# The step from attention to the merge stage, cut into channel tiles, with row splits, stores and head sums moved between stages and engines

## The chip, the cores and the metric

One core of one Trainium2 chip runs the whole program once. The metric is device time in microseconds (us), the median over executions; a profile of one further execution gives the rows that are shown. The engines are TensorE (PE; PEld is its weight load), VectorE (DVE), ScalarE (ACT), GpSimd (POOL) and SyncE (SP), which here only issues transfers.

## The reference, cut to what matters

A decoder block: sixteen meta tokens are put ahead of 2048 tokens of 1024 channels; a convolution branch and an attention branch are computed from the same projection, merged, and followed by a mixture of experts. The stages around the change compute this:

```python
a = silu(layernorm(a, ln_g, ln_b))          # convolution branch, 512 channels
y_conv = a @ w_conv_out + b_conv_out
o = forgetting_attention(q, k, v, logf).reshape(B, L, 512)   # 8 heads of 64
y_attn = o @ w_attn_out
merged = sigmoid(gate_c) * y_conv + sigmoid(gate_a) * y_attn
```

The layer norm runs over the 512 channels of a token. The attention's softmax is divided out late: the attention stage leaves unscaled head outputs and, per head and token, the sum of the exponentials, whose reciprocal scales the heads in the merge stage.

## The kernel before, in words

The program is five stages, one after the other: project, attend, merge, route, experts. A stage is a block with one instruction stream per engine; the next block begins when all engines have left it. Engines wait for each other by semaphores, in the order in which the code issues the instructions. Float32 products are made of two halves: a matrix is split into a high half (rounded for TensorE, on ScalarE) and a low half (the rest, on VectorE), and `pair_matmuls` makes three matmuls of one product (lines 92 to 94).

**Attend** (`stage_attend`). Four pairs of heads, each with 32 units (two heads by 16 query tiles of 128 tokens), each unit in groups of up to 512 keys. Per group TensorE transposes the probabilities (`turn`), ScalarE copies the high half (`high`), VectorE subtracts the low half (`low_part`), and three groups later TensorE multiplies by the values (`times_values`). At every second unit ScalarE copies a finished output (`take_output`) and GpSimd adds its two halves and, once per head, stores it to `o_d` in DRAM. The last pair's last four units (28 to 31; 3, 2, 3 and 3 groups) have no further scores to make, and into them is laid the layer norm of the first chunk of 512 tokens of the convolution branch, which lies in `conv` as four channel tiles of 128 x 512: `means` on TensorE gives the mean, VectorE subtracts it, ScalarE squares, `means` gives the variance, ScalarE takes the root, VectorE the reciprocal in two parts (line 1322). After the last group VectorE inverts the row sums (line 1332), TensorE turns them, VectorE scales all of `conv` at once (1334), ScalarE applies SiLU tile by tile (1272) and copies the high half of all four tiles (1276), and VectorE subtracts the low half (1339). SP stores the inverted sums and waits for that store.

**Merge** (`stage_merge`). Four chunks of 512 tokens. A chunk is 16 products (`PRODUCTS`) of 12 matmuls each: eight for `y_conv` (from `s_hi`, `s_lo`) and eight for `y_attn` (from `o_hi`, `o_lo`), into four PSUM banks in turn; the first four products of the first chunk go row block by row block (`first_products`). The eight row blocks of the two weights (`w_rooms`) are split at the start: `high(k)` on ScalarE (1515), `low(k)` on VectorE (1567). VectorE takes each product through its gate (`gated`, 1577, 1582, 1584), which frees its bank. Between these takes it works for what comes next, by a schedule written by hand over the product number i: `heads_and_halves` adds the two halves of the head outputs loaded from `o_d` (`add_heads`, 1590), scales them (1595) and splits off the low half (1600) for this chunk; `statistics` makes the layer norm of the next chunk's `conv`: sum over the four channel tiles by one strided reduction (`sum_tiles`, 1608), TensorE's `mean` (1459), `centre`, the square's sum, `invert`, `scale`, and at i = 13 `low_conv` for all four tiles. SP loads the heads of the next chunk at i = 7 and its `conv` at i = 13. GpSimd does nothing in this stage but one subtraction in its last chunk (2369).

## Time and profile before

| | |
|---|---|
| device time, 3 runs | median 2576.16 us (2573.84 to 2580.01) |
| the profiled execution | 2576.4 us; its span, first to last instruction, 2574.8 us |
| mean granted TensorE clock | 0.98 of full |
| busy share of the span | PE 95%, PEld 78%, DVE 73%, ACT 42%, POOL 20% |
| merge stage, first to last matmul | 1386.56 to 1591.96 us from the start of the span |

PE's busy share counts matmuls that wait in its pipeline, so it overstates TensorE. Times in the rows are counted from the start of the span. In a timeline the bracket says how long the engine sat idle before the row, and what ended that.

### The profile page before, as it was taken

How to read it: one execution, taken by the hardware profiler on the slowest of the kernel's cores; microseconds unless marked ns; L12 is line 12 of the kernel's file. 1: busy time of each engine (PE TensorE's matmuls, PEld its weight loads, DVE VectorE, ACT ScalarE, POOL GpSimd, SP SyncE). 2: the span in 40 equal slices, each digit the busy share in tenths (PEclk: the TensorE clock that was granted, in tenths of full speed). 3: DMA queues.
4: the chain of work that ended last, by engine and by line, in shares of the span. 5: the costliest groups of instructions: out<-in, count | busy, mean ns of one | idle time of the engine just before them, and what ended most of it. 6: DMA issues, size and time to landing. Idle time of an engine off the chain costs nothing. (4 is left out here: it accounts for less than half of the span.)

```text
span 2574.8 us, 33570 instructions
## 1 busy us (share of the span) xinstructions
PE 2440.4 (95%) x12296; PEld 2002.0 (78%) x12296; DVE 1881.9 (73%) x2422; ACT 1072.7 (42%) x1556; POOL 515.2 (20%) x477
## 2 busy tenths in 40 slices
PE   6999999999999999999996899999399999999998
PEld 6899898999988888989884777777367777677664
DVE  7699999799311078888886776466588888888773
ACT  6101001455212167878774222323255555555540
POOL 1222212111101101111110001011324443233221
PEclk9999999999999999999998999999699999999999
DMA  5111112232325153364424677536389999999986
GB/s 174 41 58 58 66 47 68 83 124 83 122 91 159 49 150 100 103 171 109 118 83 123 192 212 250 199 132 232 135 314 358 372 364 366 371 371 369 360 319 202
DMA packets 180273, 469.86 MB, mean 182 GB/s; under 512 B 33573, under 2 KB 104579, under 8 KB 145548
## 3 DMA queue, kind: packets, MB, share of 16 engines
q1 hardware_dynamic: 133202, 371.64, 42.4%
q0 software_dynamic: 31120, 49.48, 5.7%
q10 hardware_dynamic: 15794, 46.67, 4.8%
q8 instruction: 96, 1.57, 0.3%
q14 instruction: 61, 0.50, 0.1%
HBM read 408.65 MB, written 118.29 MB: 205 GB/s over the span
## 5 line engine op out<-in xcount | busy, mean ns | idle before, releaser
L92 PE MATMUL project_bank<-project_xnT_hi,project_w_hi 128*128 128x512 f32 (+4 forms) x1352 | 499.6, 370 | 0.7 <-DVE project_work L796 0.6
L93 PE MATMUL project_bank<-project_xnT_lo,project_w_hi 128*128 128x512 f32 (+4 forms) x1352 | 498.2, 368 | 0.0
L94 PE MATMUL project_bank<-project_xnT_hi,project_w_lo 128*128 128x512 f32 (+4 forms) x1352 | 496.4, 367 | 0.0
L809 DVE SCALAR_TENSOR_TENSOR project_work<-project_work,project_taps 128x2048 f32<-128x2048 f32 x128 | 335.5, 2621 | 4.5
L92 PEld LDWEIGHTS project_bank<-project_xnT_hi,project_w_hi 128*128 128x128 f32 (+1 forms) x1352 | 251.2, 186 | 29.8 <-issue 1.5
L94 PEld LDWEIGHTS project_bank<-project_xnT_hi,project_w_lo 128*128 128x128 f32 (+1 forms) x1352 | 251.3, 186 | 26.6
L93 PEld LDWEIGHTS project_bank<-project_xnT_lo,project_w_hi 128*128 128x128 f32 (+1 forms) x1352 | 251.1, 186 | 26.6
L2736 PE MATMUL experts_y_bank<-weights_down,experts_hT 128*128 128x512 f32 x544 | 245.9, 595 | 0.6 <-ACT experts_hT L2789 0.6
L1302 DVE TENSOR_TENSOR attend_pT<-attend_t_bank,attend_pT 128x512 fp32r<-128x512 f32 (+3 forms) x352 | 213.8, 613 | 35.4 <-ACT attend_pT L1236 34.5
L1169 PE MATMUL attend_o_bank<-attend_pT,attend_values 128*128 128x256 f32 x1216 | 225.2, 304 | 6.7 <-DVE attend_pT L1302 6.7
L1236 ACT ACTIVATE attend_pT<-attend_t_bank 128x512 fp32r<-128x512 f32 (+3 forms) x352 | 184.2, 539 | 89.6 <-PE attend_t_bank L1155 86.8
L92 PE MATMUL experts_gu_bank<-weights_high,experts_xT_hi 128*128 128x512 f32 x512 | 215.1, 420 | 6.6 <-DVE weights_low L2379 4.2
L595 ACT ACTIVATE project_work<-project_bank,project_params 128x512 f32<-128x512 f32 x64 | 44.0, 690 | 393.3 <-PE project_bank L94 393.3
L93 PE MATMUL experts_gu_bank<-weights_low,experts_xT_hi 128*128 128x512 f32 x512 | 202.6, 396 | 0.0
L94 PE MATMUL experts_gu_bank<-weights_high,experts_xT_lo 128*128 128x512 f32 x512 | 201.8, 394 | 0.0
L2379 DVE TENSOR_TENSOR weights_low<-weights_room,weights_high 128x2048 fp32r<-128x2048 f32 x86 | 193.0, 2284 | 0.0
L1155 PE MATMUL attend_t_bank<-first_ident,attend_probs 128*128 128x128 f32 x1216 | 190.3, 273 | 0.8 <-DVE attend_pT L1302 0.3
L2736 PEld LDWEIGHTS experts_y_bank<-weights_down,experts_hT 128*128 128x128 f32 x544 | 103.4, 191 | 105.4 <-issue 98.9
L407 POOL CAST project_w_hi<-project_w_raw 128x1024 fp32r<-128x1024 f32 (+1 forms) x35 | 44.4, 1267 | 697.9 <-PE project_bank L94 697.9
L2778 ACT ACTIVATE experts_xT_hi<-experts_x_bank 128x1024 fp32r<-128x1024 f32 x64 | 65.7, 1027 | 277.9 <-PE experts_x_bank L2697 277.9
L1169 PEld LDWEIGHTS attend_o_bank<-attend_pT,attend_values 128*128 128x128 f32 x1216 | 167.8, 190 | 9.2 <-DVE attend_pT L1302 8.6
L1155 PEld LDWEIGHTS attend_t_bank<-first_ident,attend_probs 128*128 128x128 f32 x1216 | 148.6, 140 | 25.1 <-issue 3.9
(320 smaller groups left out, 4693.9 us busy)
## 6 DMA issues: line engine op xcount, KB each, us to landing
weights_down<-in_w_down_dram SPq DMA_DIRECT2D x68, 1024.0 KB, 9.0
weights_room<-in_w_gate_dram SPq DMA_DIRECT2D x45, 1024.0 KB, 9.6
weights_room<-in_w_up_dram SPq DMA_DIRECT2D x45, 1024.0 KB, 14.4
weights_third<-in_w_gate_dram SPq DMA_DIRECT2D x23, 1024.0 KB, 9.7
weights_third<-in_w_up_dram SPq DMA_DIRECT2D x23, 1024.0 KB, 14.6
project_w_raw<-in_w_in_dram SPq DMA_DIRECT2D x36, 512.0 KB, 4.4
qk_d<-project_work SPq DMA_DIRECT2D x16, 1032.0 KB, 5.4
gate_d<-project_work ACTq DMA_DIRECT2D x16, 1024.0 KB, 4.2
```

The source lines that it names most:

```text
L92: pe.matmul(out, lhs[0], rhs[0], start=first, stop=False)
L93: pe.matmul(out, lhs[0], rhs[1], start=False, stop=False)
L94: return pe.matmul(out, lhs[1], rhs[0], start=False, stop=last)
L407: nc.gpsimd.tensor_copy(w_hi[:, b, :, 0:width], w_raw[:, b, :, 0:width]).then_inc(w_hi_ready, 1)
L809: nc.vector.scalar_tensor_tensor(out=work[:, 2, 0:SEQ], in0=work[:, 1, META - 1 + q:META - 1 + q + SEQ], scalar=taps[:, bass.ds(ct, 1), q] ...
L1155: m = nc.tensor.transpose(t_bank[:, j % 3, (t % 4) * P:(t % 4 + 1) * P], probs[:, u % BUF, t * P:(t + 1) * P], ident[:, :])
L1169: m = nc.tensor.matmul(out, values[:, h, t, :], pT[:, j % (LAG + 1), t % 4].rearrange("p k q -> p (k q)"), start=t == 0, stop=t == last)
L1236: nc.scalar.activation(pT[:, j % (LAG + 1), 0:n, 0, :], t_bank[:, j % 3, 0:n * P].rearrange("p (t q) -> p t q", q=P), ACT.Copy)\
L1302: nc.vector.tensor_tensor(pT[:, j % (LAG + 1), 0:n, 1, :], t_bank[:, j % 3, 0:n * P].rearrange("p (t q) -> p t q", q=P), raw(pT[:, j % (LA ...
L2379: nc.vector.tensor_tensor(self.low[n % 2][:, cut, :, :].rearrange("p c k n -> p k c n"), self.gate_up_rooms[n % 3][:, :, cut, :], raw(self ...
L2736: m = nc.tensor.matmul(y_bank[:, b, half, :], hT[:, b, c, :], down_raw[r][:, c, cols], start=c == 0, stop=c == HC - 1)
L2778: nc.scalar.activation(xT_hi[:, b, :, :], x_bank[:, :, :].rearrange("p k (c t) -> p (k c) t", t=P), ACT.Copy).then_inc(x_hi_ready, 1)
```

## The change

- **Tail of attention.** The first chunk's centring and squaring come one or two groups earlier, the variance's `means` one group later; the row sums are inverted at unit 29 and turned at unit 31; the reciprocal of the root comes in four parts instead of two. ScalarE and VectorE split weight rows 0 and 1 in units 29 and 30.
- **Seam.** The scaling, SiLU, high half and low half of the first chunk go by channel tile. Only tile 0 is scaled in the attend block; the rest is in the merge block, among the splits of weight rows 2 and 3, and each matmul row block waits for its own tile.
- **Stores.** The last pair's last two sums and the last store of `o_d` go from the attend block into the merge block on GpSimd; the store of the inverted sums is no longer waited for in attend. In merge SP waits for these stores, then loads the heads, and the next `conv` after them instead of ahead.
- **Merge chunks.** GpSimd adds the heads' halves in all four chunks. The strided reduction becomes two additions (128 x 1024 and 128 x 512). Scaling and low half go by tile. In the first chunk the statistics move from products 0 to 13 to products 7 to 15 and their two `mean` matmuls from among the convolution products to among the head products; the next `conv` is loaded at i = 15. In later chunks the first sum moves from i = 0 to i = 1.

```diff
+    def high_w(self, nc, k):
+        nc.scalar.activation(self.w_hi[:, k, :], self.w_rooms[k % 6], ACT.Copy).then_inc(self.w_hi_ready, 1)
+
+    def low_w(self, nc, k):
+        nc.vector.tensor_tensor(self.w_lo[:, k, :], self.w_rooms[k % 6], raw(self.w_hi[:, k, :]), ALU.subtract)\
+          .then_inc(self.w_ready, 1)
+
+    def scale_tile(self, nc, t, inv_root):
+        nc.vector.tensor_tensor(self.conv[:, t, :], self.conv[:, t, :], inv_root, ALU.mult).then_inc(self.scaled, 1)
...
-            sp.dma_start(inv_d.rearrange("h (t q) -> (h t) q", q=P), inv_rows[:, :]).then_inc(inv_stored, 16)
-            wait(sp, inv_stored, 16)
+            sp.dma_start(inv_d.rearrange("h (t q) -> (h t) q", q=P), inv_rows[:, :]).then_inc(merge.inv_stored, 16)
...
+            with pool.Fori(0, PAIRS - 1) as it:
+                sums(it, UNITS)
...
+            sums(PAIRS - 1, UNITS - 2)
...
+                    if not more and (u, g) == (UNITS - 1, 0):
+                        pe.wait_ge(inv_done, 1)
+                        nc.tensor.transpose(s_bank[:, 2, 0:P], inv_sum[:, :], ident[:, :]).then_inc(inv_done, 1)
+                    if not more and (u, g) == (UNITS - 2, 1):
                         pe.wait_ge(merge.squared, 1)
...
-                    if not more and (u, g) == (UNITS - 3, 0):
+                    if not more and (u, g) == (UNITS - 4, 1):
...
+                    if not more and (u, g) in ((UNITS - 3, 1), (UNITS - 2, 0)):
+                        wait(act, merge.w_loaded[u - (UNITS - 3)], 16)
+                        merge.high_w(nc, u - (UNITS - 3))
+                    if not more and (u, g) == (UNITS - 2, 0):
                         wait(act, merge.var_done, 1)
...
-            wait(act, merge.param_loaded, 48)
...
-            m.then_inc(merge.silu_done, 1)
-            wait(act, merge.silu_done, 1)
-            nc.scalar.activation(merge.s_hi[:, :, :], merge.conv[:, :, :], ACT.Copy).then_inc(merge.s_hi_ready, 1)
...
+                    if not more and (u, g) == (UNITS - AHEAD, 0):
+                        dve.wait_ge(merge.mean_done, 1)
+                        nc.vector.tensor_tensor(merge.conv[:, :, :], merge.conv[:, :, :],
+                                                over_channels(s_bank[:, 0, :]), ALU.subtract)\
+                          .then_inc(merge.centred, 1)
                     low_part(it, u, g)
...
-                    if not more and u == UNITS - 1 and g < 2:
+                    if not more and (u, g) == (UNITS - 3, 1):
+                        dve.wait_ge(exp_done, PAIRS * UNITS + 2)
+                        nc.vector.reciprocal(inv_sum[:, :], row_sum[:, :]).then_inc(inv_done, 1)
+                    if not more and (u, g) == (UNITS - 2, 0):
+                        for k in range(2):
+                            wait(dve, merge.w_hi_ready, k + 1)
+                            merge.low_w(nc, k)
+                    if not more and (u, g) in INVERT_AT:
+                        n = INVERT_AT.index((u, g))
                         dve.wait_ge(merge.root_ready, 1)
-                        nc.vector.reciprocal(inv_root[:, 256 * g:256 * (g + 1)], root[:, 256 * g:256 * (g + 1)])\
+                        nc.vector.reciprocal(inv_root[:, P * n:P * (n + 1)], root[:, P * n:P * (n + 1)])\
...
-            dve.wait_ge(exp_done, PAIRS * UNITS + 2)
-            nc.vector.reciprocal(inv_sum[:, :], row_sum[:, :]).then_inc(inv_done, 1)
-            dve.wait_ge(merge.inv_ready, 2)
-            nc.vector.tensor_tensor(merge.conv[:, :, :], merge.conv[:, :, :], over_channels(inv_root), ALU.mult)\
...
+            dve.wait_ge(merge.inv_ready, 4)
+            merge.scale_tile(nc, 0, inv_root)
             dve.wait_ge(inv_done, 2)
-            nc.vector.tensor_copy(inv_rows[:, :], t_bank[:, 0, 0:P]).then_inc(inv_done, 1)
-            dve.wait_ge(merge.s_hi_ready, 1)
-            nc.vector.tensor_tensor(merge.s_lo[:, :, :], merge.conv[:, :, :], raw(merge.s_hi[:, :, :]), ALU.subtract)\
-              .then_inc(merge.s_lo_ready, 1)
+            nc.vector.tensor_copy(inv_rows[:, :], s_bank[:, 2, 0:P]).then_inc(inv_done, 1)
...
-            wait(sp, merge.s_lo_ready, 1)
-            merge.load_conv(sp, 1)
-            load_heads(0)
             for k in (6, 7):
                 wait(sp, w_ready, k - 5)
                 merge.load_w(sp, k)
+            wait(sp, merge.inv_stored, 16)
+            for s in merge.o_stored:
+                wait(sp, s, 16 * PAIRS)
+            load_heads(0)
+            wait(sp, merge.s_lo_ready, CT)
+            merge.load_conv(sp, 1)
...
+                    if i == PRODUCTS - (1 if first else 3) and more and not (isinstance(c, int) and c == TC - 2):
+                        wait(sp, merge.s_lo_ready, c * CT + 2 * CT)
...
+                    if i == 0:
+                        pe.wait_ge(merge.s_lo_ready, c * CT + (j + 1))
                     m = part(i, j, r, hi, lo)
...
-                    if t == 3 and more:
+                    if t == 3 and more and not first:
...
+                    if t == 1 and first:
+                        mean(1, 0, merge.mean_done)
+                    if t == 4 and first:
+                        mean(2, 1, merge.var_done)
...
+            tiles, o_raw, o_sb, o_tile = merge.last_sums
+            for n, i in enumerate(tiles):
+                halves = o_raw[:, 2 * P * n:2 * P * (n + 1)]
+                nc.gpsimd.tensor_tensor(o_sb[:, i * P:(i + 1) * P], halves[:, 0:P], halves[:, P:2 * P], ALU.add)\
+                  .then_inc(o_sums, 1)
+            wait(pool, o_sums, 2)
+            pool.dma_start(o_tile, o_sb.rearrange("p (c n) -> p c n", n=512)).then_inc(merge.o_stored[1], 16)
+
+            for c in range(TC):
+                wait(pool, o_loaded, c * 96 + 96)
+                for half in range(2):
+                    s = slice(2 * half, 2 * half + 2)
+                    nc.gpsimd.tensor_tensor(o_top[:, s, :], o_top[:, s, :], o_low[:, s, :], ALU.add)\
+                      .then_inc(o_added, 1)
...
+            def conv_tile(c, t):
+                wait(act, merge.scaled, c * CT + (t + 1))
+                nc.scalar.activation(conv[:, t, :], conv[:, t, :], ACT.Silu, bias=merge.ln[:, 1, t:t + 1],
+                                     scale=merge.ln[:, 0, t:t + 1]).then_inc(merge.silu_done, 1)
+                wait(act, merge.silu_done, c * CT + (t + 1))
+                nc.scalar.activation(s_hi[:, t, :], conv[:, t, :], ACT.Copy).then_inc(merge.s_hi_ready, 1)
...
-                    square(c + 1)
+                square(c + 1)
...
+                wait(act, y_done, c * PRODUCTS + DC)
...
-                wait(act, y_done, c * PRODUCTS + DC)
-                nc.scalar.activation(s_hi[:, :, :], conv[:, :, :], ACT.Copy).then_inc(merge.s_hi_ready, 1)
-
-            for k in range(6):
+                    conv_tile(c + 1, t)
+
+            wait(act, merge.param_loaded, 48)
+            conv_tile(0, 0)
+            conv_tile(0, 1)
+            high(2)
+            conv_tile(0, 2)
+            high(3)
+            conv_tile(0, 3)
+            for k in range(4, W_CHUNKS):
...
-                nc.vector.tensor_reduce(over_tiles[:, :], source[:, :, :].rearrange("p t n -> p n t"), AX.X, ALU.add)\
+                nc.vector.tensor_tensor(squares[:, 0:2, :], source[:, 0:2, :], source[:, 2:4, :], ALU.add)\
+                  .then_inc(tiles_summed, 1)
+                wait(dve, merge.inv_ready, n // 2 + 3)
+                wait(dve, tiles_summed, n * 2 - 1)
+                nc.vector.tensor_tensor(over_tiles[:, :], squares[:, 0, :], squares[:, 1, :], ALU.add)\
...
+                wait(dve, merge.inv_ready, c + 4)
+                for t in range(CT):
+                    merge.scale_tile(nc, t, inv_root[:, :])
+
+            def low_conv(c, t):
+                wait(dve, merge.s_hi_ready, c * CT + (t + 1))
+                nc.vector.tensor_tensor(s_lo[:, t, :], conv[:, t, :], raw(s_hi[:, t, :]), ALU.subtract)\
                   .then_inc(merge.s_lo_ready, 1)
...
-                    if i in (4, 5):
-                        add_heads(0, i - 4)
-                        scale_heads(0, i - 4)
-                    elif i == 6:
-                        low(CT + 2)
-                        low(CT + 3)
-                    elif i == 7:
+                    if i == 3:
+                        for half in range(2):
+                            scale_heads(0, half)
+                    elif i == 5:
                         low_heads(0, 0)
...
-                    add_heads(c, i - 1)
                     scale_heads(c, i - 1)
...
-                if i == 0 and not first:
+                if i == (7 if first else 1):
                     sum_tiles(conv, merge.conv_loaded, c * 16 + 32, c * 2 + 1)
-                elif i == (1 if first else 3):
+                elif i == (9 if first else 3):
                     centre(c + 1)
-                elif i == (3 if first else 5):
+                elif i == (10 if first else 5):
                     sum_tiles(squares, merge.squared, c + 2, c * 2 + 2)
-                elif i == 8:
+                elif i == (12 if first else 8):
                     invert(c + 1)
-                elif i == 9:
+                elif i == (13 if first else 9):
                     scale(c + 1)
+                elif first and i >= 14:
+                    low_conv(1, 2 * i - 28)
+                    low_conv(1, 2 * i - 27)
                 elif i == 13:
-                    low_conv(c + 1)
+                    for t in range(CT):
+                        low_conv(c + 1, t)
 
...
-            for k in range(CT):
+            for t in range(1, CT):
+                merge.scale_tile(nc, t, merge.first_inv_root)
+            low_conv(0, 0)
+            low_conv(0, 1)
+            for k in (2, 3):
                 low(k)
+                low_conv(0, k)
+            for k in range(CT, W_CHUNKS):
+                low(k)
+            for s in merge.o_stored:
+                wait(dve, s, 16 * PAIRS)
```

## Rows read from the trace of the kernel before

**Rows 1.** PE's timeline over the merge stage: last attention product, waits, first matmuls of chunks.
```profile
1371.80 0.58 PE L1169 MATMUL attend_o_bank<-attend_pT,attend_values 128*128 128x256 f32 x1 [1.07 <-DVE attend_pT L1302]
...
1386.56 0.77 PE L92 MATMUL merge_y_bank<-merge_s_hi,merge_wm_hi 128*128 128x512 f32 x1 [13.43 <-DVE merge_wm_lo L1567]
...
1421.17 0.80 PE L92 MATMUL merge_y_bank<-merge_o_hi,merge_wm_hi 128*128 128x512 f32 x1 [8.17 <-DVE merge_o_lo L1600]
...
1445.03 0.40 PE L92 MATMUL merge_y_bank<-merge_s_hi,merge_wm_hi 128*128 128x512 f32 x1
...
1470.36 1.12 PE L1459 MATMUL merge_stat_bank<-merge_over_tiles,merge_mean_w 128*128 128x512 f32 x2 [1.97 <-DVE merge_over_tiles L1608]
...
1493.13 0.40 PE L92 MATMUL merge_y_bank<-merge_s_hi,merge_wm_hi 128*128 128x512 f32 x1
...
1522.25 2.07 PE L1459 MATMUL merge_stat_bank<-merge_over_tiles,merge_mean_w 128*128 128x512 f32 x2 [4.02 <-DVE merge_over_tiles L1608]
...
1547.63 0.40 PE L92 MATMUL merge_y_bank<-merge_s_hi,merge_wm_hi 128*128 128x512 f32 x1
...
1591.57 0.39 PE L94 MATMUL merge_y_bank<-merge_o_hi,merge_wm_lo 128*128 128x512 f32 x1
```

**Rows 2.** Windows view, seam: engine busy times and counts, granted clock, DMA share, GB/s.
```profile
1380.00:1390.00 10.00, 3.44 (x8) 2.79 (x9) 7.06 (x6) 6.77 (x7) 0.00 (x0) 0.50 0.54 163
```

**Rows 3.** Timeline, DVE and ACT, from attention's end to the next stage's first split.
```profile
1372.52 2.23 DVE L1334 TENSOR_TENSOR merge_conv<-merge_conv,attend_scores 128x2048 f32<-128x2048 f32 x1
...
1374.82 1.28 ACT L1272 ACT_TABLE_LOAD   x1 [1.75 <-DVE merge_conv L1334]
...
1376.12 2.93 ACT L1272 ACTIVATE merge_conv<-merge_conv,merge_ln 128x512 f32<-128x512 f32 x4
...
1379.08 1.91 ACT L1276 ACTIVATE merge_s_hi<-merge_conv 128x2048 fp32r<-128x2048 f32 x1
1381.02 2.29 DVE L1339 TENSOR_TENSOR merge_s_lo<-merge_conv,merge_s_hi 128x2048 fp32r<-128x2048 f32 x1 [6.08 <-ACT merge_s_hi L1276]
...
1384.14 2.00 ACT L1515 ACTIVATE merge_wm_hi<-merge_wm_raw 128x1024 fp32r<-128x1024 f32 x2 [3.16 <-PEq L985]
```

**Rows 4.** Timeline, PE and DVE, in attention's last units.
```profile
1356.71 5.40 PE L1181 MATMUL attend_s_bank<-attend_scores,merge_mean_w 128*128 128x512 f32 x8 [2.67 <-ACT attend_scores L1261]
...
1367.65 1.74 DVE L1322 RECIPROCAL attend_scores<-attend_scores 128x256 f32<-128x256 f32 x1
...
1371.51 0.23 DVE L1302 TENSOR_TENSOR attend_pT<-attend_t_bank,attend_pT 128x128 fp32r<-128x128 f32 x1
```

**Rows 5.** Groups by line, DVE in merge: busy us, mean ns, idle before.
```profile
L1608 DVE TENSOR_REDUCE merge_over_tiles<-merge_conv 128x512 f32<-128x2048 f32 x2 | 7.7, 3847 | 1.0 <-DMA merge_conv<-conv_d 1.0
L1584 DVE TENSOR_TENSOR merge_m_sum<-merge_m_sum,merge_prod_a 128x512 f32<-128x512 f32 x9 | 6.2, 692 | 0.4
L1590 DVE TENSOR_TENSOR merge_o_top<-merge_o_top,merge_room 128x1024 f32<-128x1024 f32 x4 | 4.8, 1208 | 0.0
```

**Rows 6.** POOL's timeline at the end of attention: the last sums and their store.
```profile
1373.25 2.21 POOL L1118 TENSOR_TENSOR attend_o_sb<-attend_o_raw 128x128 f32<-128x128 f32 x2 [4.71 <-ACT attend_o_raw L1244]
1376.19 0.77 POOL L1122 DMA_DIRECT2D o_d<-attend_o_sb  x1 [0.73 <-POOL attend_o_sb L1118]
```

**Rows 7.** DMA view, windows holding single issues at 1376.19, 1383.57, 1387.14: KB, us to landing.
```profile
o_d<-attend_o_sb POOLq DMA_DIRECT2D x1, 1024.0 KB, 4.4
merge_conv<-conv_d SPq DMA_DIRECT2D x1, 1024.0 KB, 5.2
merge_room<-inv_d SPq DMA_DIRECT2D x1, 512.0 KB, 16.8
```

**Rows 8.** GpSimd's large additions by group, and two tiles' minimum/median/maximum ns.
```profile
L2369 POOL TENSOR_TENSOR weights_merged_lo<-weights_merged_lo,weights_merged_hi 128x1024 fp32r<-128x1024 f32 x1 | 2.4, 2399 | 187.6 <-ACT weights_merged_hi L2365 187.6
L409 POOL TENSOR_TENSOR project_w_lo<-project_w_raw,project_w_hi x35: 317/2626/4344, 69.8 to 862.7; 128x1024 fp32r<-128x1024 f32 x34, 128x64 fp32r<-128x64 f32 x1
L809 DVE SCALAR_TENSOR_TENSOR project_work<-project_work,project_taps x128: 2350/2352/4385, 93.4 to 447.8; 128x2048 f32<-128x2048 f32 x128
```

84 lines of the change are left out of this document (24 added, 60 removed).

## The prediction

> **What bounds the kernel now.** I read four views: the windows and PE's timeline to find where TensorE stands still, the other engines' timelines to see who releases it, the groups by line for durations, the DMA view for loads that moved. Four things are to be seen.
>
> First, between the last attention product at 1371.80 and the first merge matmul at 1386.56 TensorE has one small transpose to do [rows 1]. The chain is serial, over whole 128 x 2048 tiles: scaling 2.23, table load 1.28, four SiLUs 2.93, high half 1.91, low half 2.29 us, then the change of block, from 1383.31 to ScalarE's first split at 1384.14, 0.83 us [rows 3], then the first row's split.
>
> Second, in the first chunk TensorE finishes its convolution products at 1413.00 and waits 8.17 us for the heads' low half until 1421.17 [rows 1].
>
> Third, chunk lengths. The last chunk, which prepares no successor, runs from 1547.63 to 1591.96: 44.3 us, so 0.231 us a matmul. The others take 58.5, 48.1 and 54.5 us. Chunks 1 and 2 stop for the sum over channel tiles, 1.97 and 4.02 us [rows 1], behind reductions of 3.85 us on VectorE [rows 5]. Chunk 1 less its wait is 46.1, which is the 44.3 plus 1.8 for two `mean`s.
>
> Fourth, the clock. After a stop the granted clock is 0.50 of full, the 1.2 GHz level [rows 2], and the first matmuls come at half pace: the eight head products of the first chunk, restarted at 1421.17, take 23.9 us to 1445.03 instead of 22.2 [rows 1].
>
> Everything after merge waits for it by events, so I carry a gain at the last merge matmul through to the end.
>
> **The change, part by part.** I follow one time line, in us of the trace.
>
> *Tail.* The centring moves into a stretch in which VectorE is idle, and the row sums' reciprocal moves ahead of the last groups. Against that VectorE gets two splits of about 1.2 us (a row of the same size [rows 5]), and ScalarE two high halves of 1.0 [rows 3]. They lie beside `means`, which takes 5.40 us from 1356.71 [rows 4]; TensorE has nothing for them to do then. After `means`, VectorE's chain is five low parts (about 2.7 us in all) and four reciprocals of half the 1.74 us [rows 4], about 6.3 us, beginning 1.4 us after `means`. With `means` starting at about the same 1356.8 and taking 3.7 us at full clock or 5.4 at half, the last low part ends between 1368 and 1369.8, against 1371.74 now [rows 4]. Tile 0's scaling (a quarter of 2.23) and the copy of the inverted sums follow, beside the last output's copy. The merge block begins at 1370.8 (bounds 1369.8 and 1372.5, the latter if nothing of the tail is saved).
>
> *Seam.* What is left ahead of the first matmul: table load 1.28, one SiLU 0.73, one high half a quarter of 1.91 and some start-up, 0.55, one low half 0.6, hops 0.2. The first row's split is done already. 1370.8 + 3.4 = 1374.2, against 1386.56: 12.3 us (bounds 10.5 and 13.5). Tiles 1 to 3 and rows 2 and 3 come from ScalarE in turns of about 1.3 and 1.0 us, while TensorE spends at least 2.8 us, and 5.1 at half clock, on a row block: covered, the last tile is there at about 1381. Without that cover each tile would cost its 1.3.
>
> One rule of the Trainium skill (ScalarE: Activation LUTs, What ACT_TABLE_LOAD costs) adds a drain of 1.38 us to each table load. The rows show the SiLU starting 0.02 us after the load's 1.28, and the load 0.07 us after its releaser [rows 3]; with the page's figure the first matmul would stand at 1375.6. The sum goes by the row.
>
> *The heads.* The old order had the store out at 1376.19, landed 4.4 later, and loads from 1383.94 behind a `conv` load [rows 6, 7]. Now GpSimd's two sums begin with the block: 0.9 to 2.2 us [rows 6] (2.2 where VectorE scales meanwhile; I take 1.5), 0.7 to the issue, 4.4 to landing: 1377.5. SP's issues then queue behind this wait: six head loads, then `conv`, and with it the first gates. The two weight loads go out first and land before 1377. The head loads: `conv` landed at 1383.57 + 5.2 = 1388.8, the last head load at 1387.14 + 16.8 = 1403.9, so 3 MB took 15.1 us [rows 7]. From 1377.8, with 2 us of start-up, they land at 1395 (bounds 1393 and 1398).
>
> Then two GpSimd additions of 128 x 1024. The same form took 2.40 us where VectorE did other things, 2.63 at the median and up to 4.34 in the project stage [rows 8]. I take 2.4 here (VectorE waits idle for them) up to 3.2: 1399.8. Scaling two halves, high halves, two takes and two low halves, 1.2 us each, follow on VectorE: 6.3 us. The head products start at 1406 (bounds 1403 and 1409), against 1421.17. TensorE ends its convolution products at 1374.2 plus the old 26.4 us less two `mean`s, 1.8: 1398.8, so it stands still for 7 us here, and the slow clock after it stays as it was.
>
> *End of the first chunk.* 1406 + 23.9 + 1.8 for the `mean`s moved here = 1431.7. But the statistics of chunk 1 are now compressed into products 7 to 15. I followed them: takes of 1.4 us (twice 0.69 [rows 5]), centre 2.3, square 1.9, sum 1.9, root, reciprocal 3.5, scaling 2.3 bring the scaled tile 0 to about 1430, SiLU and high half of it to 1432, and the low halves of tiles 0 to 3 to 1434 to 1438.5 between two takes. TensorE, waiting tile by tile, loses 4.8 us (bounds 2 and 8). Chunk 1's effective start is 1436.5, against 1445.03: 8.5 us ahead.
>
> *Chunks 1 and 2.* VectorE loses the additions, 2 x 1.21, and 2 x (3.85 - 1.9) of reductions [rows 5]: 6.3 us of about 40 a chunk. The waits of 1.97 and 4.02 go, and in chunk 2 the slow clock behind the second: ideal is 46.1 each. Against that stand GpSimd's additions. The DVE operation with two SBUF inputs that takes 2.35 us at the median took up to 4.39 while GpSimd made its additions [rows 8]: each side can hold the other for up to one operation. Here the loads land near the end of a chunk, where VectorE makes the next chunk's low halves. Two additions of 2.4 can hold it for 0 to 4.8 us; I take 1.3 on TensorE's path. Chunk 2's `conv` lands late as before and costs 0.6. So 47.4 and 48.0: gains 0.7 and 6.5. Chunk 3 stays 44.3.
>
> *Sum.* 8.5 + 0.7 + 6.5 = 15.7, so 16 us. The profiled 2576.4 less 16 is 2560.4; its distance to the median of 2576.16 is 0.2 us, nothing here. A change under 0.2%, 5 us, counts as none.
>
> **Rivals.**
>
> *The chain holds everywhere (0.22).* No boundary stall beyond 2 us at chunk 1 and no interference: 8.5 + 2.8 + 2.0 + 8.4 = 21.7, to 2555. For it: the tile-wise waits let TensorE start on tile 0. Against it: the compressed statistics above.
>
> *GpSimd and VectorE hold each other (0.16).* Additions take 3.2 us, so the heads come 1.6 us later, and the starts of chunks 1 and 2 lose 3.2 us each beyond the sum: 16 - 8 = 8, to 2568. For it: the 4.39 and 4.34 [rows 8]. Against it: many VectorE operations in merge read PSUM and one SBUF operand. [...]
>
> *The other side (0.05).* GpSimd's eight additions fall on the path throughout. At the longest row, 4.34, they cost 34.7 where VectorE spent 9.7 [rows 5, 8]: 25 us lost against the 21.7, slower by 3, to 2580. It decides from 3.9 us an addition, with all eight on the path. Against it: six of the eight are requested long before their sums are used.
>
> *The change gains nothing (0.04).* The stage's start could still hang on something that this trace hides behind the VectorE chain, as the barrier's wait for the store of the sums, landing at 1380.6 [rows 6, 7]; with the heads late behind it, 2574 to 2578.
>
> **How the numbers follow.** My forecast has 0.53, at 2560.4, its own range 2555.5 to 2565. The range of 2552 to 2569 takes in the first two rivals and the bounds: best case 13.5 - 12.3 + 21.7 = 23, with 1 for run to run; worst 8 less 1. It leaves out some 0.15. Faster by over 0.2% 0.91, within 0.04, slower 0.05.
>
> **What the changed profile would show.** The first merge matmul comes near 1374.2, some 5 us behind the last attention product instead of 14.8. The head products start near 1406 with a wait named for VectorE's `o_lo` and behind it GpSimd's additions. Chunk 1 begins with waits on single `s_lo` tiles, 3 to 6 us in sum. Chunks 1 and 2 last 47 to 48 us with no wait of 4 us for the channel sum and no half clock. GpSimd's additions last 2.4 us, and some of VectorE's tile operations (0.6) are stretched to 2 or 3. The prediction is wrong if the head loads land after 1400, if the barrier is later than 1373, or if the stretch at the chunk boundaries exceeds 5 us each.

## The result, and the profile after

The changed kernel takes 2562.39 us in the median of 7 runs (2556.7 to 2569.27), the kernel before, beside it on the same chip, 2578.75 us (7 runs, 2573.84 to 2582.92). The ratio is 0.9938, with a 95% interval of 0.9923 to 0.9953: 0.6% faster. The profiled execution took 2561.39 us with a span of 2559.6, against the 2574.8 of before, so the trace shows 15.2 of the 16 us. The forecast was 2560.4 us, 15.7 less than before.

PE's timeline of the changed kernel, with the rows that answer to [rows 1] and [rows 4]:

```profile
1356.84 3.60 PE L1204 MATMUL attend_s_bank<-attend_scores,merge_mean_w 128*128 128x512 f32 x8
...
1367.37 0.58 PE L1192 MATMUL attend_o_bank<-attend_pT,attend_values 128*128 128x256 f32 x1 [0.26 <-DVE attend_pT L1320]
...
1373.11 0.77 PE L92 MATMUL merge_y_bank<-merge_s_hi,merge_wm_hi 128*128 128x512 f32 x1 [5.16 <-DVE merge_s_lo L1670]
...
1405.17 0.80 PE L92 MATMUL merge_y_bank<-merge_o_hi,merge_wm_hi 128*128 128x512 f32 x1 [7.50 <-DVE merge_o_lo L1641]
...
1434.83 0.50 PE L92 MATMUL merge_y_bank<-merge_s_hi,merge_wm_hi 128*128 128x512 f32 x1 [4.42 <-DVE merge_s_lo L1670]
...
1437.97 0.80 PE L92 MATMUL merge_y_bank<-merge_s_hi,merge_wm_hi 128*128 128x512 f32 x1 [0.28 <-DVE merge_s_lo L1670]
...
1484.51 0.40 PE L92 MATMUL merge_y_bank<-merge_s_hi,merge_wm_hi 128*128 128x512 f32 x1
...
1530.35 0.40 PE L92 MATMUL merge_y_bank<-merge_s_hi,merge_wm_hi 128*128 128x512 f32 x1
...
1533.79 0.50 PE L92 MATMUL merge_y_bank<-merge_s_hi,merge_wm_hi 128*128 128x512 f32 x1 [1.18 <-DVE merge_s_lo L1670]
...
1575.74 0.39 PE L94 MATMUL merge_y_bank<-merge_o_hi,merge_wm_lo 128*128 128x512 f32 x1
```

The stop at the seam is 5.16 us instead of 13.43, and the waits for the channel sums are gone: 1.97 in chunk 1, 4.02 in chunk 2, and one of 1.46 in chunk 2 that [rows 1] leave out. The stop ahead of the head products is still there, 7.50 us for 8.17, and a new one of 4.42 us stands at chunk 1's first matmul. The last merge matmul ends at 1576.13.

The seam on ScalarE and VectorE, as [rows 3] of before, timeline view:

```profile
1367.23 0.68 DVE L973 TENSOR_TENSOR merge_conv<-merge_conv,attend_decay 128x512 f32<-128x512 f32 x1
...
1369.52 1.28 ACT L1562 ACT_TABLE_LOAD   x1 [0.87 <-PEq L1003]
1370.81 0.81 ACT L1562 ACTIVATE merge_conv<-merge_conv,merge_ln 128x512 f32<-128x512 f32 x1
1371.66 0.63 ACT L1565 ACTIVATE merge_s_hi<-merge_conv 128x512 fp32r<-128x512 f32 x1
...
1372.32 0.69 DVE L1670 TENSOR_TENSOR merge_s_lo<-merge_conv,merge_s_hi 128x512 fp32r<-128x512 f32 x1 [0.92 <-ACT merge_s_hi L1565]
```

One tile's chain, 1.28, 0.81, 0.63 and 0.69 with short hops, is all that stands ahead of the first matmul. GpSimd's timeline shows the sums and the store, as in [rows 6], and then its additions of the heads' halves:

```profile
1368.94 1.31 POOL L1537 TENSOR_TENSOR attend_o_sb<-attend_o_raw 128x128 f32<-128x128 f32 x2 [4.21 <-POOLq L1003]
1370.55 0.77 POOL L1540 DMA_DIRECT2D o_d<-attend_o_sb  x1 [0.30 <-POOL attend_o_sb L1537]
1394.61 4.70 POOL L1546 TENSOR_TENSOR merge_o_top<-merge_o_top,merge_room 128x1024 f32<-128x1024 f32 x2 [23.28 <-DMA merge_room<-inv_d]
1425.29 5.20 POOL L1546 TENSOR_TENSOR merge_o_top<-merge_o_top,merge_room 128x1024 f32<-128x1024 f32 x2 [25.99 <-DMA merge_room<-inv_d]
1482.48 5.50 POOL L1546 TENSOR_TENSOR merge_o_top<-merge_o_top,merge_room 128x1024 f32<-128x1024 f32 x2 [51.98 <-DMA merge_room<-inv_d]
1527.76 5.42 POOL L1546 TENSOR_TENSOR merge_o_top<-merge_o_top,merge_room 128x1024 f32<-128x1024 f32 x2 [39.79 <-DMA merge_room<-inv_d]
```

VectorE at the same times, timeline view:

```profile
1397.03 4.50 DVE L1636 TENSOR_TENSOR merge_o_top<-merge_o_top,merge_room 128x1024 f32<-128x1024 f32 x2 [9.63 <-POOL merge_o_top L1546]
...
1422.99 3.35 DVE L1661 RECIPROCAL merge_ln_inv_root<-merge_over_tiles 128x512 f32<-128x512 f32 x1
1426.26 0.63 DVE L1628 TENSOR_TENSOR merge_prod_a<-merge_y_bank,merge_room 128x512 f32<-128x512 f32 x1
1426.92 1.32 DVE L1630 TENSOR_TENSOR merge_m_sum<-merge_m_sum,merge_prod_a 128x512 f32<-128x512 f32 x1
1428.17 4.68 DVE L973 TENSOR_TENSOR merge_conv<-merge_conv,merge_ln_inv_root 128x512 f32<-128x512 f32 x4
...
1481.02 4.70 DVE L1670 TENSOR_TENSOR merge_s_lo<-merge_conv,merge_s_hi 128x512 fp32r<-128x512 f32 x4
```

The head loads landed at 1394.61, and GpSimd's additions begin there. VectorE operations with two operands in SBUF are longer beside them: two scalings of heads take 4.50 us where one took 1.23 before (eight took 9.8), the addition at 1426.92 takes 1.32 for 0.69, and four scalings of tiles take 4.68. The reciprocal (one operand) and the product from PSUM (0.63) keep their length beside the same addition. The Trainium skill (SBUF — State Buffer, Who interferes with whom) says just this: an operation with two SBUF inputs contends with GpSimd's reads, and one with at most one does not, outside VectorE's two-port modes. The rows agree on both.

### The profile page after: what moved, and what is told of

The parts are those of the page before. It is cut to its first block and busy times, and to the rows that moved or that the text cites. A ratio compares the mean times of both kernels' runs of the same rounds, so it can differ in the third digit from the quotient of the medians.

```text
span 2559.6 us, 33615 instructions
## 1 busy us (share of the span) xinstructions
PE 2439.0 (95%) x12296; PEld 2002.0 (78%) x12296; DVE 1876.7 (73%) x2446; ACT 1074.6 (42%) x1568; POOL 543.5 (21%) x485
```

## The experiments

The table has times of the profiled executions in us after the last attention product (1371.80 before, 1367.37 after), since the stretch ahead of it, the same code in all, shifts by up to 3.6 us from run to run. Its columns are the first matmul of merge, of the first chunk's head products, of chunks 1, 2 and 3, the end of the last merge matmul, and the median and ratio to the kernel before with its 95% interval. The kernel before had medians of 2579.05 us beside 1 to 4, 2580.24 beside 5, 6, 7 and 9, and 2579.47 beside "changed, again", "7 again" and 8.

| | merge | heads | chunk 1 | 2 | 3 | end | median | ratio |
|---|---|---|---|---|---|---|---|---|
| before | 14.8 | 49.4 | 73.2 | 121.3 | 175.8 | 220.2 | 2578.75 | 1 |
| changed | 5.7 | 37.8 | 67.5 | 117.1 | 163.0 | 208.8 | 2562.39 | 0.9938 [0.9923, 0.9953] |
| changed, again | 5.7 | 37.2 | 67.4 | 115.2 | 161.0 | 206.8 | 2562.14 | 0.9933 [0.9921, 0.9946] |
| 1 additions on VectorE | 5.7 | 35.4 | 63.1 | 112.9 | 160.2 | 204.5 | 2559.83 | 0.9926 [0.9910, 0.9943] |
| 2 strided sum | 5.7 | 37.4 | 67.7 | 117.4 | 166.0 | 211.7 | 2565.42 | 0.9943 [0.9926, 0.9959] |
| 3 all tiles first | 11.7 | 37.5 | 67.3 | 116.0 | 161.8 | 207.6 | 2560.03 | 0.9921 [0.9904, 0.9937] |
| 4 rows in merge | 7.2 | 41.0 | 71.3 | 119.2 | 166.5 | 212.2 | 2563.00 | 0.9932 [0.9915, 0.9948] |
| 5 two additions alone | 14.8 | 47.4 | 72.1 | 118.0 | 169.0 | 213.3 | 2570.03 | 0.9959 [0.9943, 0.9975] |
| 6 table load ahead | 5.7 | 37.2 | 67.7 | 116.5 | 162.3 | 208.0 | 2561.63 | 0.9928 [0.9913, 0.9944] |
| 7 heads by half | 5.7 | 32.7 | 58.1 | 106.7 | 154.0 | 198.3 | 2555.77 | 0.9912 [0.9897, 0.9927] |
| 7 again | 5.7 | 33.0 | 60.0 | 109.4 | 156.7 | 201.1 | 2558.00 | 0.9918 [0.9905, 0.9931] |
| 8 halves, statistics earlier | 5.7 | 32.7 | 58.0 | 109.5 | 157.0 | 201.3 | 2554.99 | 0.9904 [0.9890, 0.9918] |
| 9 as 8, table load ahead | 5.7 | 34.2 | 59.8 | 111.4 | 159.0 | 203.3 | 2559.94 | 0.9922 [0.9909, 0.9936] |

The changed kernel's two profiles differ by 2 us, all of it in chunk 1: a single profile's sum is good to about that, and the argument goes by the waits. The profile is one execution of each kernel, and not always a middle one: it is the fastest in 7 (2548.22 us), 7 again (2553.88) and 9 (2554.92), the slowest in 4 (2566.34) and 8 (2558.54).

**Changed, again.** The same kernel, as a yardstick for 7 again and 8, which ran on the same chip.

> The changed kernel once more, beside the two kernels of this call and on the same chip, so that their medians can be set against it. Theory: 2560 to 2564 us, ratio to the kernel before 0.993 to 0.995, last merge matmul about 204.8 us after the last attention product plus 4 (first merge matmul to last matmul 203.0 us, as in its first profile).

The median came out as expected. From first to last merge matmul it was 201.1 us, 1.9 fewer than 203.0, and the windows view says why; after the five engines' busy times come the granted clock, the DMA share and GB/s. First the changed kernel's first profile, then the second:

```profile
1436.00:1438.00 2.00, 1.68 (x4) 0.86 (x4) 1.88 (x3) 1.97 (x3) 0.00 (x0) 0.50 0.03 11
1438.00:1440.00 2.00, 2.00 (x5) 1.61 (x6) 0.69 (x1) 0.00 (x0) 0.00 (x0) 0.50 0.85 223
1440.00:1442.00 2.00, 2.00 (x7) 1.52 (x6) 0.75 (x1) 0.00 (x0) 0.00 (x0) 0.50 1.02 367
```

```profile
1436.00:1438.00 2.00, 1.98 (x5) 0.90 (x3) 1.97 (x4) 1.94 (x4) 0.00 (x0) 0.52 0.14 42
1438.00:1440.00 2.00, 1.81 (x7) 1.35 (x8) 0.83 (x2) 0.22 (x1) 0.00 (x0) 1.00 0.77 193
```

After stops of 4.42 and 3.61 us at about the same place, the clock stood at 1.2 GHz until past 1442 in the one and until 1438 in the other. GpSimd's hold differed too. VectorE's timeline of the second profile:

```profile
1427.95 2.72 DVE L1630 TENSOR_TENSOR merge_m_sum<-merge_m_sum,merge_prod_a 128x512 f32<-128x512 f32 x1
1430.59 2.48 DVE L973 TENSOR_TENSOR merge_conv<-merge_conv,merge_ln_inv_root 128x512 f32<-128x512 f32 x4
```

Here one addition of a product was held, 2.72 for 0.69, and the tile scalings behind it took 2.48.

**1. The head additions back on VectorE**, rest as changed.

```diff
-            for c in range(TC):
-                wait(pool, o_loaded, c * 96 + 96)
-                for half in range(2):
...
-                    nc.gpsimd.tensor_tensor(o_top[:, s, :], o_top[:, s, :], o_low[:, s, :], ALU.add)
+                            add_heads(0, half)
...
+                    add_heads(c, i - 1)
```

> The changed kernel with the head halves' additions back on VectorE in all four chunks, all else kept. My theory (GpSimd's additions are longer, 4.7 to 5.5 us a pair, and hold VectorE's two-input operations): the head products start 1.9 us earlier, near 1403.3 instead of 1405.17, VectorE's four scaling tiles in the first chunk take 2.5 us instead of 4.68, the stop ahead of chunk 1 shrinks from 4.42 to 1.5 to 2.5 us, the stop of 1.18 in chunk 3 goes; chunks 1 and 2 lose at most 1 us each at the second channel sum. In all 3 to 5 us faster than the changed kernel in the merge stage. Rival (VectorE needed the relief): the waits for the channel sums come back with 2 us or more each in chunks 1 and 2, and the stage ends 2 to 4 us later than in the changed kernel.

The end came 4.3 us sooner than in the first profile of the changed kernel and 2.3 sooner than in the second. Timeline, VectorE in this run:

```profile
1394.58 1.23 DVE L1630 TENSOR_TENSOR merge_o_top<-merge_o_top,merge_room 128x1024 f32<-128x1024 f32 x1 [7.16 <-DMA merge_room<-inv_d]
1395.84 1.23 DVE L1635 TENSOR_TENSOR merge_o_top<-merge_o_top,merge_room 128x1024 f32<-128x1024 f32 x1
...
1426.30 2.49 DVE L973 TENSOR_TENSOR merge_conv<-merge_conv,merge_ln_inv_root 128x512 f32<-128x512 f32 x4
```

An addition is 1.23 us here, 2.35 on GpSimd; the tile scalings are 2.49, and from the end of the reciprocal to the end of the tile scalings it is 3.7 us, against 6.5 and 5.7 in the changed kernel's two profiles, whichever operation was held there. The first chunk gains: the heads start 1.8 to 2.4 us sooner, and the stop ahead of chunk 1 is 1.58 us (with 0.26 and 0.96 behind it) instead of 4.42. Chunk 1 lasts 49.8 us, in the changed kernel 49.7 and 47.75. Later it is even: chunk 2 lasts 47.3 us against 45.8, with waits for channel sums back (1.70 in chunk 1 and 1.16 in chunk 2, where at most 1 was expected), and chunk 3 44.3 against 45.8, without GpSimd's hold. So by the profiles moving the additions to GpSimd lost 2 to 4 us, all in the first chunk. The medians (2559.83 and 2562.39, not measured together) point the same way, but their intervals overlap.

**2. The strided reduction back in place of two additions**, rest as changed.

```diff
-                nc.vector.tensor_tensor(squares[:, 0:2, :], source[:, 0:2, :], source[:, 2:4, :], ALU.add)
...
-                nc.vector.tensor_tensor(over_tiles[:, :], squares[:, 0, :], squares[:, 1, :], ALU.add)
+                nc.vector.tensor_reduce(over_tiles[:, :], source[:, :, :].rearrange("p t n -> p n t"), AX.X, ALU.add)
```

> The changed kernel with each sum over channel tiles as one strided reduction again (3.85 us instead of 1.9). My theory: the first chunk's statistics are a chain on VectorE, so both sums count there (3.9 us more ahead of chunk 1), and chunks 1 and 2 wait 2 to 3 us each for the second sum: 8 to 10 us later at the end of merge. Rival (the sums lie in VectorE's slack): under 2 us.

It lost 3.0 to 4.9 us by the profiles and 3.0 by the medians (whose intervals overlap), less than the 8 to 10 expected. 2.7 of them are chunk 2, 48.5 us instead of 45.8, with mean waits of 1.38 and 0.79. Up to chunk 2's start the reductions cost 0.3 to 2.3 us: in this profile GpSimd's additions fell on the reciprocal, which has one operand and kept its length, and on one addition (1.36 for 0.69), and the tile scalings behind them took 2.48.

**3. The first matmul waits for all four tiles**, rest as changed.

```diff
-                    pe.wait_ge(merge.s_lo_ready, j + 1)
+                    pe.wait_ge(merge.s_lo_ready, CT)
```

> The changed kernel with TensorE's first matmul waiting for all four channel tiles instead of tile 0 alone. The first merge matmul moves from 1373.1 to 1379.1. My theory now: the head products are released by the chain store, load, addition, scaling, not by TensorE, so they start at 1405.2 as before, the 7.5 us stop ahead of them shrinks to 1.5, and the end of merge stays or comes up to 2 us earlier, since the clock does not fall. Rival (the seam's 12 us were earned by the early first matmul): the end comes 6 us later.

PE's timeline of this run, whose last attention product is at 1370.03, 2.7 us later than in the changed kernel:

```profile
1381.72 0.76 PE L92 MATMUL merge_y_bank<-merge_s_hi,merge_wm_hi 128*128 128x512 f32 x1 [11.30 <-DVE merge_s_lo L1670]
...
1407.50 0.50 PE L92 MATMUL merge_y_bank<-merge_o_hi,merge_wm_hi 128*128 128x512 f32 x1 [1.59 <-DVE merge_o_lo L1641]
...
1437.31 0.80 PE L92 MATMUL merge_y_bank<-merge_s_hi,merge_wm_hi 128*128 128x512 f32 x1 [5.94 <-DVE merge_s_lo L1670]
```

The first matmul is 6.0 us later by the table, the head products are where they were (37.5; 37.8 and 37.2 in the changed kernel), and so is all that follows. The wait moved from the one stop to the other, 7.50 to 1.59. What times the first chunk is the chain store, head loads, additions, scaling; TensorE's own early start is slack there. Chunk 1's start hangs on VectorE as well: the head products ran at full clock after the short stop and ended 1.7 us sooner, counted from the last attention product, but the stop behind them was 5.94 us instead of 4.42, since GpSimd's additions held the tile scalings for longer here (6.85 us for four).

**4. Weight rows 0 and 1 split in merge**, rest as changed.

```diff
-                        merge.high_w(nc, u - (UNITS - 3))
...
-                            merge.low_w(nc, k)
+            high(0)
...
+            low(0)
```

> The changed kernel with weight rows 0 and 1 split in merge again. My theory: attention's last matmul stays where it was within 0.5 us, since the splits lay where VectorE waited for means and root; the first merge matmul comes 1 to 2 us later; the head products and everything after stay within 1 us. Rival (the splits in the tail were worth their own 4.5 us, or cost the tail as much): the end of merge moves by over 2 us.

A miss in the profile: the first matmul lost 1.5 us as expected, but the head products 3.2 to 3.8, and the end 3.4 to 5.4. The medians (2563.00 and 2562.39) don't show such a loss, and the profile is the slowest of the four executions; so the chain that follows is shown, its size is not. SP's timeline, first in this run, then in the changed kernel:

```profile
1374.57 2.65 SPq L980 DMA_DIRECT2D merge_wm_raw<-in_w_attn_out_dram  x2
1377.32 0.50 SPq L1416 DMA_DIRECT2D merge_o_top<-o_d  x1
```

```profile
1368.90 0.81 SPq L980 DMA_DIRECT2D merge_wm_raw<-in_w_attn_out_dram  x2
1376.35 0.50 SPq L1423 DMA_DIRECT2D merge_o_top<-o_d  x1
```

The loads of weight rows 6 and 7 go into the rooms of rows 0 and 1, so they wait for those rows' low halves. Here they are issued 5.7 us later, just ahead of the head loads on the same queue, and the heads land at 1397.94 instead of 1394.61. The head loads themselves go out only 1.0 us later (1377.32 for 1376.35), so 2.3 of the 3.3 us are longer flight. What the splits in attention's tail buy seems to be not so much their own time as a head start of 7.4 us for 1 MB of loads, which otherwise goes out just ahead of the head loads; no run moves these loads alone.

**5. The kernel before, with two additions in place of the strided reduction**, with the count that TensorE waits for, nothing else.

```diff
+                nc.vector.tensor_tensor(squares[:, 0:2, :], source[:, 0:2, :], source[:, 2:4, :], ALU.add)
...
-                nc.vector.tensor_reduce(over_tiles[:, :], source[:, :, :].rearrange("p t n -> p n t"), AX.X, ALU.add)
+                nc.vector.tensor_tensor(over_tiles[:, :], squares[:, 0, :], squares[:, 1, :], ALU.add)
```

> The kernel before with one part of the change alone: each sum over channel tiles as two additions instead of one strided reduction. My theory: the stops of 1.97, 1.46 and 4.02 us go and chunks 1 and 2 last 46 to 47 us instead of 48.1 and 54.5, so 9 us there; in the first chunk only the second sum is on the way to the heads, 2 us: 9 to 11 us earlier at the end of merge, so in the kernel before this part alone would have brought over half of the change's gain. Rival (the sums are worth what the changed kernel showed when they were put back): 3 us.

By the profile it lies between the two expectations, 6.9 us from the last attention product on. By the medians it is the first one: 10.2 us (ratio 0.9959, interval 6.5 to 14.7 us), over half of the change's gain. In the profile chunk 1 starts 1.1 us sooner (the head products 1.9), chunk 1 itself is 2.3 shorter without its wait of 1.97, and chunk 2 takes 51.0 us instead of 54.5. It still stopped for `mean` there, 0.54 and 2.48 us: VectorE sat idle 5.74 us for `conv`, until 1500.73, and had the heads' work besides. One row ahead of merge matters for the comparison. PE's timeline of this run, whose code is that of before up to there:

```profile
1359.61 3.70 PE L1181 MATMUL attend_s_bank<-attend_scores,merge_mean_w 128*128 128x512 f32 x8 [2.66 <-ACT attend_scores L1261]
```

After the same stop (2.67 in [rows 4]) `means` took 3.70 us here and 5.40 there: the clock stayed at 1.00 in this execution.

**6. ScalarE's wait for the convolution buffer put ahead of its wait for the variance**, so that nothing stands between the root and SiLU's table load.

```diff
+                wait(act, y_done, c * PRODUCTS + DC)
...
-                wait(act, y_done, c * PRODUCTS + DC)
```

> The changed kernel with ScalarE's wait for the convolution products moved from behind the root to ahead of it, so that only one wait stands ahead of the first SiLU of a chunk. My theory: in the first chunk the table load then runs before the wait for the scaled tile, and the stop of 4.42 us ahead of chunk 1 shrinks by 1.3 us to 3.1; the end of merge comes 1.3 to 2 us earlier. Rival (the low halves are held by VectorE's order, not by ScalarE): nothing moves by over 0.5 us.

ScalarE's timeline, changed kernel first, then this one:

```profile
1417.98 1.28 ACT L1590 ACT_TABLE_LOAD   x1
1422.26 0.69 ACT L1590 ACTIVATE merge_over_tiles<-merge_stat_bank,merge_ln_eps 128x512 f32<-128x512 f32 x1 [3.00 <-PE merge_stat_bank L1482]
1431.12 1.28 ACT L1562 ACT_TABLE_LOAD   x1 [8.16 <-DVE merge_conv L973]
```

```profile
1423.51 1.28 ACT L1591 ACT_TABLE_LOAD   x1 [4.34 <-PE merge_stat_bank L1482]
1424.81 0.69 ACT L1591 ACTIVATE merge_over_tiles<-merge_stat_bank,merge_ln_eps 128x512 f32<-128x512 f32 x1
1425.51 1.28 ACT L1562 ACT_TABLE_LOAD   x1
```

With one wait ahead of the root its table load ran before the wait, and SiLU's, with two waits ahead, after them. The edit swapped the two: the 1.28 us only changed places, and the end moved by no more than the changed kernel's two profiles differ. The 1.3 to 2 us of the theory did not come.

**7. As 1, with the first chunk's heads loaded half after half**, each half with its own semaphore.

```diff
+                for half in range(2):
+                    s = slice(2 * half, 2 * half + 2)
...
+                        sp.dma_start(o_top[part, s, :], o_d[h, 0, 0:HD, s, :]).then_inc(o_first[half], 16)
...
-            load_heads(0)
+            load_first_heads()
```

> The changed kernel with the additions on VectorE, and the first chunk's heads loaded in two halves one behind the other (12 transfers instead of 6), so that the first half is added and scaled while the second lands. My theory (store, load, addition and scaling of the heads set the end of the first chunk): against the run with the additions on VectorE alone the head products start 2 to 4 us earlier, near 1400, and the end of merge comes 2 to 4 us earlier. Rival (smaller transfers are slower, or SP's 12 issues are the bound): the last half lands over 2 us later and nothing is gained.

> Head additions on VectorE and the first chunk's heads loaded in two halves, once more. Its first run had 192.6 us from first merge matmul to last where the changed kernel has 203.0 and the additions-on-VectorE kernel 198.8. Theory (half the heads earlier gives head products 3 to 5 us earlier, and a short stop leaves the clock up): 193 to 196 us again, median 5 to 8 us below the changed kernel of this call. Rival (that profile was a lucky one; the clock falls in other executions): 196 to 199 us and the median within 4 us of it.

PE's timeline of the first run, and the clock's windows behind it:

```profile
1399.66 0.50 PE L92 MATMUL merge_y_bank<-merge_o_hi,merge_wm_hi 128*128 128x512 f32 x1 [1.81 <-DVE merge_o_lo L1654]
```

```profile
1399.00:1401.00 2.00, 1.34 (x6) 1.11 (x7) 2.00 (x4) 0.00 (x0) 0.00 (x0) 1.00 0.54 209
1401.00:1403.00 2.00, 2.00 (x11) 1.65 (x10) 1.90 (x3) 0.00 (x0) 0.00 (x0) 1.00 0.50 106
```

The first half is added and scaled while the second still flies. The head products start 2.5 to 2.8 us sooner than in 1, and the end comes 3.4 (second run) to 6.2 us sooner (first). The first run's stop, 1.81 us, left the clock at 1.00; the second's, 3.04 us, was followed by 0.50 until about 1404. That is most of the difference of the two. Against the changed kernel on the same chip the median is 4.1 us lower, a little short of the 5 to 8 expected, and the ratios' intervals overlap. Both profiles caught the fastest execution of their kernel, so the sums of the table flatter it.

**8 and 9. As 7, with chunk 1's statistics one product earlier**; 9 also has the edit of 6.

```diff
-                    if t == 1 and first:
+                    if t == 0 and first:
...
-                if i == (7 if first else 1):
+                if i == (6 if first else 1):
```

> As the kernel with halves, with chunk 1's statistics one product earlier, without the table load moved. In the run that had both, the stops of 1.58, 0.25 and 0.95 us ahead of chunk 1 became 0.20 and 0.88, but a stop of 2.21 us came at chunk 1's first channel sum. Theory A (that stop is the later conv load's, and the Sqrt's table load ate the rest): 191 to 194 us from first merge matmul to last, 1 to 2 us below the halves alone. Theory B (products 6 to 12 hold no room on VectorE before the second half of the heads is in): 195 to 199 us, 2 us or more above the halves alone.

> Additions on VectorE, heads by halves, the table load ahead, and the first chunk's statistics one product earlier. My theory: the head products start near 1400, the stops ahead of chunk 1, 1.6 + 0.3 + 1.0 with additions on VectorE alone, go almost entirely, and merge ends 6 to 9 us earlier than with additions on VectorE alone, near 1565: about 11 us under the changed kernel, 2551 to 2554 in all. Rival (VectorE is the bound of the first chunk whatever the order): the stops turn up elsewhere in the chunk, and under 3 us are gained.

The stops ahead of chunk 1 shrank from 1.59, 0.25 and 0.96 (7 again) to one of 0.61, but the next wait ate it. PE's timeline of 8:

```profile
1443.26 1.13 PE L1493 MATMUL merge_stat_bank<-merge_over_tiles,merge_mean_w 128*128 128x512 f32 x2 [2.38 <-DVE merge_over_tiles L1664]
```

VectorE waited there for chunk 2's `conv`, which landed at 1441.14. That is 70.6 us after the last attention product, and 70.4 in 7 again (1438.03): the load, not the schedule, sets this sum. Of expectation A the cause held (the new stop is the load's), but not its 191 to 194 us from first to last merge matmul: it was 195.6 against 195.4 in 7 again. That is in B's range, though not the 2 us above the halves that B adds. Here the slowest execution of 8 stands beside the fastest of 7 again; the medians differ by 3.0 us in favour of 8, so the sum of 8 is one execution's. By the medians 8 is the best version, 2554.99 us, 7.2 below the changed kernel on the same chip, and here the two intervals do not overlap; nor do the runs tell it from 7. In 9 the second half of the heads landed late (1395.82, against 1394.47 in 7 again and 1393.54 in 7), and its first matmuls came at half clock after a stop of 3.84; that one run doesn't show whether the table load added to it. Its expectation, 6 to 9 us ahead of 1 in merge, was a miss: 1.2 us by the table, nothing by the medians (2559.94 and 2559.83).

## Why the prediction was right

**The times of the chain.** Predicted and measured, in us of the trace:

| | before | predicted | after |
|---|---|---|---|
| merge block's begin (ScalarE) | 1384.1 | 1370.8 | 1369.5 |
| first merge matmul | 1386.56 | 1374.2 | 1373.11 |
| head loads landed | 1403.9 | 1395 | 1394.6 |
| head products | 1421.17 | 1406 | 1405.17 |
| chunk 1 (effective start) | 1445.03 | 1436.5 | 1438.4 |
| chunk 2 | 1493.13 | 1483.9 | 1484.51 |
| chunk 3 | 1547.63 | 1531.9 | 1530.35 |
| last merge matmul | 1591.96 | 1576.3 | 1576.13 |

**Tail and seam: right, and less worth than they look.** `means` ran at full clock (3.60 us, for 5.40 in [rows 4]), and 3.6 us after the block's begin the first matmul ran (3.4 predicted). The SiLU began 0.01 us after its table load had ended, as in [rows 3]; the drain of 1.38 us that the Trainium skill (ScalarE: Activation LUTs, What ACT_TABLE_LOAD costs) adds is not in the rows. Of the 15.8 us at the last merge matmul, 4.4 were already there at the last attention product. But the full clock under `means` need not be the change's doing: in experiment 5 the old tail had it too. From the start of `means` to the last attention product it was 15.1 us before, 13.4 in experiment 5 and 10.5 in the changed kernel, so 1.7 us of the tail's gain is the luck of the one profile before. And the 13.4 us gained at the first matmul are not what counted. Experiment 3 gave 6 of them back and lost nothing: the head chain is the bound, as the 7 us stop in the forecast implies without saying so. No run takes the tail or the move of the stores back alone, so what each of them is worth stays open.

**The heads: right in sum, with errors that cancel.** The store was issued at 1370.55, 2.5 us sooner than predicted (1370.8 + 1.5 + 0.7), and took 5.7 us instead of 4.4; the loads went out at 1376.35 (1377.5 predicted) and landed at 1394.6, after 18.3 us instead of 17.5, and the additions took 4.70 for both (4.8). The scalings, priced at 1.2 each, took 4.50 for two, held by the second addition; but the first began before that addition was done, where the forecast put both behind it. Experiment 4 shows what the forecast took for granted: the row splits in the tail cost attention's last products nothing (10.5 us from `means` with and without them).

**End of the first chunk: the size was off.** The last head product ended 1.3 us sooner than forecast (1430.4 for 1431.7), and the stop was 4.42 for 4.8. Left out was the slow clock behind that stop: chunk 1 lasted 49.7 us, 3.6 more than the forecast's 46.1 without waits, 0.28 of it the second stop, so its effective start is 1438.4 by that measure. (Chunk 2, which had no wait, took 45.8, as did chunk 1 in experiment 5.) It was priced after the heads' stop and forgotten here. GpSimd's additions fell on the tile scalings (4.68 for 2.3) or, in the second profile, on the addition ahead of them, and the table load of 1.28 came after them on the path. Of the 16.0 us by which the head products came sooner, 1.4 went to the `mean`s among them and other small terms, 4.4 to the stop, and 1.6 to chunk 1's length (the slow clock, less the 1.97 wait that is gone): 8.6 are left at chunk 2.

**Chunks 1 to 3: right in sum, by errors that cancel.** That the last merge matmul came within 0.2 us of the forecast is luck: chunk 1's effective start was 1.9 us late, its own length 1.3 less than priced once the slow clock is put there, chunk 2 was 2.2 shorter and chunk 3 1.5 longer. Chunk 2 took 45.8 instead of 48.0: `conv` was in time for TensorE, and GpSimd's hold lay behind TensorE's work. Chunk 3 took 45.8 instead of 44.3: there the same hold reached TensorE, 1.18 us at 1533.79. Experiment 2 brings back part of chunk 2's stop for the channel sum, and experiment 5 shows the two additions alone to be worth 6.9 us by its profile and 10.2 by the medians. On top of the rest of the change they are worth 3.0 (experiment 2, medians): the parts' gains do not add up.

**The rivals.** "The chain holds everywhere" (21.7 us) fell at chunk 1's stop of 4.42; without the additions on GpSimd the runs come near it (15.8 + 2 to 4). "GpSimd and VectorE hold each other" (8 us left) was right in mechanism and, by experiment 1, worth 2 to 4 us where it was priced at 8, since most held operations had nobody waiting. "The other side" needed 3.9 us an addition with all eight on the path; they took 2.35 to 2.75, as means of a pair, and only the first two pairs and the last pair reached the path. "Nothing gained" is excluded by the chain's times.

## What to carry to other kernels

Cutting a seam into tiles moves the first matmul at once, but its gain is bounded by the next chain that is already running: follow that chain (here store, loads, addition, scaling) before paying for the seam, and see which loads stand ahead of it on its queue. An operation moved to an idle engine is not free if it is longer there (2.35 against 1.23) and holds the busy engine meanwhile; where it sits on the path, keep it on the faster engine. Price every stop of TensorE together with the slow clock that follows it, and halve a load whose consumer can start with half.

## What the runs showed of the hardware

- The slow clock after a stop varies from run to run: half clock until 1442 after a stop of 4.42 us that ended at 1434.83, until 1438 after 3.61 (1435.06), until about 1442 after 4.89 (1438.71, experiment 4), until about 1404 after 3.04 (1400.60, 7 again), none after 1.81 (7) or 1.59 (3). The longer stop did not always have the longer slow stretch. In the changed kernel's two profiles the slow clock behind the stop, with a small second stop, made chunk 1 longer by 3.9 and by 1.9 us (49.7 and 47.75 for the 45.8 of a chunk without waits). After stops of 2.67 and 2.66 us ahead of `means` the clock fell in one execution (0.50 at 1358 to 1360, before) and stayed at 1.00 in another (experiment 5).
- GpSimd's 128 x 1024 additions took 2.35 us each with VectorE idle or held, and 2.4 to 2.75 (mean of a pair) beside VectorE's work. Four tile operations of VectorE beside them took 4.68 and 4.70, and 6.85 in experiment 3, for 2.49, a single one 2.72 for 0.69, while those that read PSUM or one SBUF operand kept their length.
- The table load for the next function ran ahead of one wait (1417.98, with 3.00 us of idle time after it) and behind two (1431.12); moving one wait swapped which of the two loads was hidden.
